# Expert rows taken from token order and added into the output rows in place

## The reference, cut to what matters

```
h = h + hier_moe(rms_norm(h, norm_ffn_g), ...)
# hier_moe: 4 groups of 8 experts
grp    = argmax(x @ wg + bg)                        # one group for each token
top_i  = top_k(logits of that group's 8 experts, 2) # two experts, both of that group
combine = p_grp * softmax(top_v)
y[token] = sum over its two experts e of
           combine * ((silu(x @ w_gate[e]) * (x @ w_up[e])) @ w_down[e])
```

## Time and profile before

| | |
|---|---|
| median of 3 runs | 2831.09 us (2827.97 to 2831.43) |
| profiled execution, span | 2829.0 us |
| PE busy | 94% of the span |
| experts' loop in it | 2446.8 to 2780.0 us |
| behind the loop | 2780.0 to 2829.0 us |

### The profile page before, as it was taken

The page is one execution under the profiler, slowest core; times in us unless marked ns, Lnnn a source line. Parts: engine busy times, 40 slices in busy tenths (PEclk is TensorE's granted clock), DMA queues, the critical chain, the costliest instruction groups (busy, mean ns, idle before and its releaser), DMA issues. The chain is left out here.

```text
span 2829.0 us, 32119 instructions
## 1 busy us (share of the span) xinstructions
PE 2657.8 (94%) x12144; PEld 2094.4 (74%) x12144; DVE 1596.7 (56%) x2120; ACT 1200.7 (42%) x1743; POOL 338.1 (12%) x289
## 2 busy tenths in 40 slices
PE   6999999999999999999999989899999879599993
PEld 5888888888878787777777779897666658477772
DVE  5688888888641323443343333686666543666664
ACT  4234444344340213545235323564555521366661
POOL 0010111101100000000000000133122210342213
PEclk9999999999999999999999999999999989699997
DMA  5333323333245212021121131234322031999997
GB/s 188 112 123 108 108 75 108 108 108 101 75 146 196 78 49 82 30 75 43 55 74 42 49 134 34 88 120 164 113 60 56 13 92 68 364 356 347 355 353 275
DMA packets 209160, 362.65 MB, mean 128 GB/s; under 512 B 51911, under 2 KB 159816, under 8 KB 195320
## 3 DMA queue, kind: packets, MB, share of 16 engines
q1 hardware_dynamic: 193432, 322.94, 33.0%
q0 software_dynamic: 14720, 34.64, 3.2%
q10 hardware_dynamic: 864, 3.15, 0.3%
HBM read 310.72 MB, written 116.93 MB: 151 GB/s over the span
## 5 line engine op out<-in xcount | busy, mean ns | idle before, releaser
L398 PE MATMUL PS<-UHI,WHI 128*128 128x512 f32 x1008 | 415.8, 413 | 4.1 <-DVE ULO L127 4.1
L398 PE MATMUL PS<-ULO,WHI 128*128 128x512 f32 x1008 | 400.2, 397 | 0.0
L398 PE MATMUL PS<-UHI,WLO 128*128 128x512 f32 x1008 | 400.2, 397 | 0.0
L127 DVE TENSOR_TENSOR WLO<-arena,WHI 128x1024 fp32r<-128x1024 f32 x94 | 115.3, 1227 | 215.7 <-ACT WHI L123 215.6
L398 PEld LDWEIGHTS PS<-UHI,WHI 128*128 128x128 f32 x1008 | 190.6, 189 | 52.3 <-issue 5.5
L398 PEld LDWEIGHTS PS<-ULO,WHI 128*128 128x128 f32 x1008 | 190.6, 189 | 47.6 <-issue 5.5
L398 PEld LDWEIGHTS PS<-UHI,WLO 128*128 128x128 f32 x1008 | 190.2, 189 | 46.3
L1500 PE MATMUL PS<-U2HI,WHI 128*128 128x512 f32 x480 | 193.0, 402 | 2.7 <-DVE WLO L127 2.7
L1500 PE MATMUL PS<-U2HI,WLO 128*128 128x512 f32 x480 | 189.4, 395 | 0.0
L1500 PE MATMUL PS<-U2LO,WHI 128*128 128x512 f32 x480 | 189.4, 395 | 0.0
L834 DVE SCALAR_TENSOR_TENSOR RC<-arena,cols,RC 128x1024 f32<-128x1024 f32 x120 | 157.2, 1310 | 10.3 <-issue 0.9
(11 more groups left out here) (465 smaller groups left out, 6019.4 us busy)
## 6 DMA issues: line engine op xcount, KB each, us to landing
arena<-in_w_in SPq DMA_DIRECT2D x88, 512.0 KB, 3.9
xd_dram<-in_x SPq DMA_DIRECT2D x32, 768.0 KB, 6.9
y_dram<-in_x SPq DMA_DIRECT2D x32, 768.0 KB, 6.8
arena<-in_w_gate SPq DMA_DIRECT2D x13, 1024.0 KB
arena<-in_w_up SPq DMA_DIRECT2D x13, 1024.0 KB
arena<-in_w_down SPq DMA_DIRECT2D x13, 1024.0 KB, 13.7
qk_dram<-RA SPq DMA_DIRECT2D x32, 384.0 KB, 2.3
arena<-qk_dram SPq DMA_DIRECT2D x32, 384.0 KB, 4.4
```

The costliest lines, as they stand in the source:

```text
L127: return eng.tensor_tensor(dst, src, hi.bitcast(F32), ALU.subtract)
L398: last = pe.matmul(o[:, h * HALF:(h + 1) * HALF], x[:, k, :], y[:, k, h * HALF:(h + 1) * HALF], start=(k == r == 0), stop=(k == ND - 1 and ...
```

## The change

The normalised rows XN are stored in token order (`xn_dram`), and the residual rows straight into the output (`out_rows`). A one-hot row (rank of the pair against 0..127) times the token's number, multiplied on PE with the one-hot matrix of picked experts and summed over the tokens, gives the token number of each slot of each expert (`id_rows`, `ids`, `id_sum`, in `SLOTI`), and the same with the shares gives each slot's share (`share_rows`, `slot_shares`, in `CSLOT`; 16 matmuls in block 1). There is no scatter of rows. `rows_in` gathers a block's rows from `xn_dram`, into one of two buffers, and `base` gathers the same tokens' rows of the output into YB; DVE adds share times the block's result to them (`result`, in place of ACT's `store`), and `rows_out` writes them back. The experts are taken in an order in which four blocks in a row belong to four groups, so that no token stands in two of them; the spare block is the 29th (`SPARE` = 28). The list of pairs for spare blocks is written in blocks 7 to 14. The final gathers, sums and stores, and the 64 fills, are gone.

```diff
-                def fill(n):
-                    size = 2 * NBLK * P // NFLAT
-                    dst, at = (xd_dram, y_dram)[n // (NFLAT // 2)], n % (NFLAT // 2) * size
-                    sp.dma_start(dst[at:at + size, :], a["x"][0, n % 5 * size:(n % 5 + 1) * size, :]
-                                 ).then_inc(s_filled, 16)
...
-                sp.wait_ge(s_filled, 16 * NFLAT)
...
+        BATCHES = (0, 3), (3, 6), (6, 8)
+        SPARE = 28
+        LISTING = 7
+        def expert_of(b):
+            n = b if b < SPARE else b - 1
+            return n % NGRP * EPG + n // NGRP
...
                     r = b % NRW
-                    if b == 0:
+                    if b < 2:
                         sp.wait_ge(s_h2p, NT)
-                    elif b == 1:
-                        sp.wait_ge(s_scat, 16 * 2 * NT)
+                    elif b < 4:
+                        sp.wait_ge(s_xland[b - 2], 16)
                     elif b < NRW:
-                        sp.wait_ge(s_xland[b - 2], 16)
+                        sp.wait_ge(s_xnst, 16 * NT)
+                        sp.wait_ge(s_h2st[0], 16 * NT // 2)
+                        sp.wait_ge(s_h2st[1], 16 * NT // 2)
                     else:
                         sp.wait_ge(s_down, b - NRW + 1)
-                    if b < NE:
-                        e = b
...
-                    sp.dma_start(h2_dram[m], RC[:, m, :]).then_inc(s_h2st[m % 2], 16)
+                    sp.dma_start(out_rows[m * P:(m + 1) * P, :], RC[:, m, :]).then_inc(s_h2st[m % 2], 16)
+                    sp.wait_ge(s_xn, m + 1)
+                    sp.dma_start(xn_dram[m * P:(m + 1) * P, :], XN[m]).then_inc(s_xnst, 16)
                 for b in range(NS):
                     load_weights(b)
-                sp.wait_ge(s_down, NS - 3)
-                for m in range(6):
-                    sp.dma_start(H2[m], h2_dram[m]).then_inc(s_h2land, 16)
-                sp.wait_ge(s_down, NS - 2)
-                for m in range(6, NT):
-                    sp.dma_start(H2[m], h2_dram[m]).then_inc(s_h2land, 16)
 
...
-                for m in range(NT):
-                    sp.wait_ge(s_sum, m + 1)
-                    sp.dma_start(out_rows[:, m, :], H2[m]).then_inc(s_out, 16)
-                sp.wait_ge(s_out, 16 * NT)
 
...
+                def ids(n):
+                    m0, m1 = BATCHES[n]
+                    for m in range(m0, m1):
+                        for u in range(2):
+                            k = 2 * m + u
+                            pe.wait_ge(s_idrow, k + 1)
+                            pe.matmul(PS[:, 7, 2 * P:2 * P + NE], IDROWS[k % 6], PICKS[:, u, m, :],
+                                      start=(k == 2 * m0), stop=(k == 2 * m1 - 1)).then_inc(s_ids, 1)
...
-                    act.wait_ge(s_down, b + 1)
-                    if b >= 2:
-                        act.wait_ge(s_yst[b % 2], 16 * (b // 2))
-                    act.activation(YB[b % 2], banks(6), ACT.Copy).then_inc(s_yb, 1)
 
...
+                act.wait_ge(s_h2st[0], 16 * NT // 2)
...
-                for n, (m0, m1) in enumerate(BATCHES):
-                    if n == 1:
-                        pool.wait_ge(s_h2p, NT)
-                        for k in range(3):
-                            last = pool.memset(XB[k], 0.0)
-                        last.then_inc(s_xzero, 1)
-                    pool.wait_ge(s_rows8, n + 1)
-                    for m in range(m0, m1):
-                        for u in range(2):
-                            pool.indirect_dma_start(xd_dram, bass.IndirectOffsetOnAxis(ap=ROWX[:, u, m:m + 1], axis=0),
-                                                    XN[m], None).then_inc(s_scat, 16)
...
+                def block_tokens(b):
+                    if b == SPARE:
+                        return bass.IndirectOffsetOnAxis(ap=LISTI[:, 0, 0:1], axis=0)
+                    e = expert_of(b)
                     return bass.IndirectOffsetOnAxis(ap=SLOTI[:, e:e + 1], axis=0)
 
                 def rows_in(b):
-                    if b >= 3:
-                        pool.wait_ge(s_xgt, b - 2)
-                    pool.indirect_dma_start(XB[b % 3], None, xd_dram[0:NE * P, :], used_slots(b),
-                                            bounds_check=NE * P - 1, oob_is_err=False).then_inc(s_xland[b % 3], 16)
+                    if b >= 2:
+                        pool.wait_ge(s_xgt, b - 1)
+                    if b == SPARE:
+                        pool.wait_ge(s_listed, 16)
+                    pool.indirect_dma_start(XB[b % 2], None, xn_dram, block_tokens(b),
+                                            bounds_check=T - 1, oob_is_err=False).then_inc(s_xland[b % 2], 16)
+                def base(b):
+                    if b >= 2:
+                        pool.wait_ge(s_yst[b % 2], 16 * (b // 2))
+                    pool.indirect_dma_start(YB[b % 2], None, out_rows, block_tokens(b),
+                                            bounds_check=T - 1, oob_is_err=False).then_inc(s_base[b % 2], 16)
 
                 def rows_out(b):
                     pool.wait_ge(s_yb, b + 1)
-                    if b < NE:
-                        pool.indirect_dma_start(y_dram[0:NE * P, :], used_slots(b), YB[b % 2], None,
-                                                bounds_check=NE * P - 1, oob_is_err=False).then_inc(s_yst[b % 2], 16)
-                    else:
...
+                rows_in(0)
+                rows_in(1)
                 pool.wait_ge(s_zlist, 16)
+                pool.wait_ge(s_total, 1)
+                for k in range(2):
+                    pool.wait_ge(s_h2st[k], 16 * NT // 2)
...
                 for b in range(NS):
...
-                    elif b + 3 == NE:
-                        pool.wait_ge(s_listed, 16)
-                        pool.wait_ge(s_xgt, NE - 2)
-                        gather(XB[NE % 3], LISTI[:, 0:1], s_xover)
+                    if b not in (SPARE, SPARE + 1):
+                        base(b)
+                    if b + 2 < NS:
+                        rows_in(b + 2)
                     if b:
                         rows_out(b - 1)
+                    if b in (SPARE, SPARE + 1):
+                        pool.wait_ge(s_yst[(b - 1) % 2], 16 * ((b - 1) // 2 + 1))
+                        base(b)
+                    if b == LISTING:
+                        pool.wait_ge(s_listrows, 1)
+                    if LISTING <= b < LISTING + NT:
+                        list_tokens(b - LISTING)
+                    elif b == LISTING + NT + 1:
+                        pool.wait_ge(s_listst, 16 * 2 * NT)
+                        pool.dma_start(LISTI[:], list_dram.rearrange("(b p) o -> p b o", p=P)).then_inc(s_listed, 16)
                 rows_out(NS - 1)
                 for k in range(2):
                     pool.wait_ge(s_yst[k], 16 * ((NS + 1 - k) // 2))
...
-                pool.wait_ge(s_moe, 1)
-                for m in range(NT):
-                    for u in range(2):
-                        k = 2 * m + u
-                        pool.indirect_dma_start(YGATH[k], None, y_dram,
-                                                bass.IndirectOffsetOnAxis(ap=ROWI[:, u, m:m + 1], axis=0)
-                                                ).then_inc(s_yg[k], 16)
 
...
+                def id_rows(n):
+                    m0, m1 = BATCHES[n]
+                    for m in range(m0, m1):
+                        for u in range(2):
+                            k = 2 * m + u
+                            if k >= 6:
+                                dve.wait_ge(s_ids, k - 5)
+                            dve.tensor_scalar(IDROWS[k % 6], IOTA[:], RANKU[:, u, m:m + 1], TOKEN[:, m:m + 1],
+                                              ALU.is_equal, ALU.mult).then_inc(s_idrow, 1)
+                def id_sum(n):
+                    dve.wait_ge(s_ids, 2 * BATCHES[n][1])
+                    placed = PS[:, 7, 2 * P:2 * P + NE]
+                    if n == 0:
+                        dve.tensor_scalar(SLOTSUM, placed, float(NOWHERE), None, ALU.add).then_inc(s_idsum, 1)
+                    elif n == 1:
+                        dve.tensor_tensor(SLOTSUM, SLOTSUM, placed, ALU.add).then_inc(s_idsum, 1)
+                    else:
+                        dve.tensor_tensor(SLOTI[:], SLOTSUM, placed, ALU.add).then_inc(s_slots, 1)
...
+                def share_rows(k0, k1):
+                    for k in range(k0, k1):
+                        if k >= 8:
+                            dve.wait_ge(s_shared, k - 7)
+                        u, m = k % 2, k // 2
+                        dve.tensor_scalar(SHAREROWS[k % 8], IOTA[:], RANKU[:, u, m:m + 1], CHOSEN[u][:, m:m + 1],
+                                          ALU.is_equal, ALU.mult).then_inc(s_sharerow, 1)
...
+                def result(b):
+                    dve.wait_ge(s_down, b + 1)
+                    dve.wait_ge(s_base[b % 2], 16 * (b // 2) + 16)
+                    if b == SPARE:
+                        share = LISTI[:, 0, 1:2].bitcast(F32)
 ```

(80 more changed lines are left out.)

202 lines of the change are left out of this document (93 added, 109 removed).

## The result

The changed kernel takes **2998.89 us** in the median of 4 runs (2996.89 to 3001.55), the kernel before 2830.05 in its 4 (2827.97 to 2831.43): a ratio of 1.0595, 95% interval [1.058, 1.061]. It is slower, as forecast, but 77 us slower than the forecast and outside its range. The profiled execution has a span of 2997.6 us, 168.6 more than before.

What follows compares the result with a forecast made beforehand. PE bounds the loop, idling only at both ends; the change adds a ring of waits. Start +2.6, ring +115, end -26.5 sum to +91: 2920 on the profiled 2829.0, median 2922 us; range 2855 to 2975.

Steps and rivals of the forecast that it cites:

- wake-up and base 2.1: In the loop, after a store lands: POOL wakes 0.8, issues base 1.0, and a gap 0.3, so 2.1 us.
- The fills: In the first part, dropping the 64 fills was counted as 0 us, since PE had work throughout.
- the end: From turn(29) to the program's end: 72.1 us instead of 98.6, so -26.5; no final gathers, sums or stores.
- the ring: Loop, turn(4) to turn(29): waits closing over two blocks, 29.5 us, so 14.75 a block instead of 10.14; +115 us.
- gather lands 5.3: In the loop, rows_in behind base: free value 4.3 plus 1.0 for base's rows and the next burst, 5.3 us.
- list of signs: In the loop: PE idle 3 to 5 us before transposes, stores 8 to 10, gathers 4 to 7, clock under 1.
- signs that it named for being wrong: Turn to turn staying at 10.1 us, stores landing in 4 to 5, or weights or `result` setting the block.
- the cold start taken by half: In the loop, PE's slow clock after idling: 2.0 us for one cold start, 1.0 put into the two-block sum.
- Fair turns: Rival: queues alternate in the loop, store lands in 6.6 us, 12.5 us a block; 2863 us, chance 0.14.
- free landings: Rival: in the loop store (4.4) and gather (4.3) land as if free, 11.4 us a block; 2833, chance 0.08.
- The rival in which both DMAs stay as slow as now: In the loop store 9.1, gather 10.8, each block starting cold: 36 us for two blocks; 3009 us, chance 0.11.
- The faster rival: In the loop POOL's wait ends before costing PE anything, blocks stay at 10.14 us; 2784 us, chance 0.07.

Runs made afterwards that it cites:

- rows_first: Changed kernel with POOL's order rows_in(b+2), base(b), rows_out(b-1), so the gather stands ahead of the waiting base; 2864.92 us.
- gather_early: Changed kernel, still two YB buffers, with rows_in(b+3) issued one block earlier, ahead of base(b) and rows_out(b-1); 2848.42 us.
- both_fills: Changed kernel with a third YB buffer from block 9, gather one block earlier, and 64 useless 768 KB copies in part one; 2825.04 us, 2824.46 without the copies.
- weights_later: Changed kernel with SP requesting block b's weights only once the rows of block b-1 have landed too; 2924.56 us.
- spaced: Changed kernel with 8 useless products of 384 columns on PE behind turn_hidden of blocks 2 to 28; 2970.70 us.

## Why the prediction was wrong

**Right.** The mechanism and its place: base's wait for a store, with the gather behind it in POOL's queue, slows every block. `rows_first` and `gather_early` show it by moving the gather alone. Right in size: the result 1.3, POOL's start 0.8, wake-up and base 2.1, and the store, 8.9 in the mean of the twelve pairs for a forecast 9.1. The fills at nothing (`both_fills`). Most of the end, -21.4 for -26.5: up to the last `down` it is within 1 us of the forecast (65.6 us behind turn(29) for 64.7). From there to the end it is 11.5 us (2986.1 to 2997.6), where 7.4 stood in the sum. The last store landed in 3.2 us, at 2991.4, and 6.2 us follow for which 1.0 had been put; what fills them the profile doesn't show.

**The step that failed** is one term of the ring: "gather lands 5.3". It was taken from blocks evenly 14.75 us apart, with the weight burst well ahead of the gather. The blocks don't come evenly. One wait releases two of them, so the second `down` of a pair, and its 3 MB, come 10.15 us after the first, just ahead of the time at which store and base are done and the gather starts. It landed in 10.1 in the mean. `weights_later` holds the burst and gets the gather back to 5.1 and the pair to 30.3; `spaced` makes the blocks nearly even and gets 5.2. The prediction's list of signs had gathers of 4 to 7 us and PE idle 3 to 5 us ahead of the transposes; it was 13.1 us in the mean, ahead of every other turn. None of the signs that it named for being wrong came.

**A second term**, the cold start taken by half. The transposes took 1.97 us behind each stop, as in rows 10, where warm ones take 0.90, and `gate_up` 6.1 to 7.5, 6.8 in the mean, for 5.6: 2.3 in each pair, where the sum had 1.0.

By size, in the mean of the twelve pairs: 4.8 (gather) and 1.3 (cold) less 0.2 (store) is 5.9 us of the 6.0 by which a pair is longer than 29.5. Twelve pairs make 72, and the half pair left, turn(28) to turn(29), is 2 shorter than forecast: the 70 by which the ring was missed. In the stretch ahead of turn(4) one such gather, 10.96 us, cost another 5.7, and the loop began 3 us sooner than forecast.

**The rivals.** Fair turns (2863) and free landings (2833) are refuted: the store took 8.3 to 9.5 us beside a burst, and q0 had no row in 2541:2543. The first had 6.6 for the store (7.0 by its own count of eight packets of 0.33 us). By the Trainium skill ("DMA: Bandwidth & Descriptors", Queues, rings and completion order) each DMA engine takes the rings that have work in turn, packet by packet. The rows of 2541:2543 don't look like that, as rows 7 didn't; those of 2545:2547, with 103 packets of each queue, do. Why q0 moves nothing in the first 3 us stays open. The rival in which both DMAs stay as slow as now (3009) had the sizes of both landings nearly right (9.1 and 10.8 for 8.9 and 10.1). It was set aside with the argument that a slower loop leaves the queue empty for 40% of the time. It does, at a share of 0.57, and this decided nothing: the gather that a turn waited for fell into the other 60% each time. Its words say a cold start for each block, but its 36 us hold one of 2.0 for two blocks, which is what came. It was 10 us too long, and by its pairs it is the account that fits best; it had a chance of 0.11. The faster rival (2784) was not reached even with the ring taken apart; there the landings grew to 12.8 to 17.3 us in the median.

## What to carry to other kernels

Before a wait goes into an in-order queue, list what stands behind it: here one line moved was worth 134 us of 169, and a third buffer without it 74. Where a ring of waits releases several blocks at once, draw the next round with its bursts of requests in time, and take a landing from the bursts issued just ahead of it and just behind, not from the mean share of the queues. Blocks made longer but even can beat the same blocks in pairs.

## What was unexpected

In the stalled loop the same gather from the same queue landed in 3.7 to 5.2 or in 9.0 to 11.2 us, by whether 3 MB of weights had been requested 2.1 to 3.6 us earlier or 15 and more. At a DMA share of 0.95 stores took 12.8 us, gathers 15.2 and `base` 17.3, in the median. And 139 us of added work on TensorE made the program 28 us shorter; part of that is the clock, 0.98 in the loop against 0.82 (2444:2982 of the kernel after), where each stop of 12 to 14 us cost 2.3 us of slow transposes and products behind it, in the mean.
